# Gate and up projections of a two-block transformer forward pass: two weight units taken matmul by matmul in turn instead of one after the other

## What is computed

```
def swiglu(h, w1, w3, w2):
    return (jax.nn.silu(h @ w1) * (h @ w3)) @ w2
...
x = x + c * swiglu(rmsnorm(x, gain), w1, w3, w2)      # c is 1.0 once, 0.5 four times
```

## Time and profile before

| | |
|---|---|
| median of 3 runs | 3458.57 us (3454.5 to 3460.02) |
| the profiled execution | 3455.16 us |
| its span, first to last instruction | 3453.4 us |
| TensorE matmuls | 15598, busy 3324.4 us (96% of the span) |
| TensorE weight loads | 15598 |
| VectorE busy | 1727.2 us (50%) |
| ScalarE busy | 1109.7 us (32%) |
| mean share of DMA bandwidth (queue of the weights) | 25.2% of 16 engines |
| mean granted TensorE clock | 0.987 |

### The profile page before, as it was taken

The page is one execution under the profiler, slowest core; times in us unless marked ns, Lnnn a source line. Parts: engine busy times, 40 slices in busy tenths (PEclk is TensorE's granted clock), DMA queues, the critical chain, the costliest instruction groups (busy, mean ns, idle before and its releaser), DMA issues.

```text
span 3453.4 us, 41062 instructions
## 1 busy us (share of the span) xinstructions
PE 3324.4 (96%) x15598; PEld 2730.9 (79%) x15598; DVE 1727.2 (50%) x2510; ACT 1109.7 (32%) x1482; POOL 0.2 (0%) x4
## 2 busy tenths in 40 slices
PE   7989999989999999999899999999999989999998
PEld 6667777868888888888786888888888878778886
DVE  4554444555454455435755545444443576555543
ACT  3554444343222222222333322232222233332221
POOL 0000000000000000000000000000000000000000
PEclk9999999999999999999999999999999989999999
DMA  3222222313222222232231222222222223222222
GB/s 125 86 74 92 86 80 70 107 61 116 97 97 98 97 94 95 97 101 80 74 104 61 86 97 97 98 92 97 97 98 101 80 70 108 68 79 94 95 97 86
DMA packets 88829, 313.49 MB, mean 91 GB/s; under 512 B 9984, under 2 KB 10496, under 8 KB 88448
## 3 DMA queue, kind: packets, MB, share of 16 engines
q1 hardware_dynamic: 82080, 294.69, 25.2%
q10 hardware_dynamic: 6624, 17.03, 1.6%
HBM read 309.58 MB, written 2.10 MB: 90 GB/s over the span
## 4 chain that ended last, share of the span: by engine, by line
PE 89%; DVE 5%; ACT 3%; issue 2%; DMA 0%; ACTq 0%; DVEq 0%
PE ps L827 27%; PE ps L829 27%; PE ps L828 27%; PE ps L1026 1%; PE ps L889 1%; PE ps L944 1%; PE ps L898 1%; DVE wlo L1257 1%; ACT whi L1072 1%; PE ps L973 1%; PE ps L934 1%; PE ps L957 0%; PE ps L1056 0%; PE ps L926 0%; PE ps L977 0%
## 5 line engine op out<-in xcount | busy, mean ns | idle before, releaser
L827 PE MATMUL ps<-x_hi,whi 128*128 128x512 f32 x2816 | 1118.0, 397 | 13.1 <-DVE wlo L1257 13.1
L829 PE MATMUL ps<-x_hi,wlo 128*128 128x512 f32 x2816 | 1101.9, 391 | 0.0
L828 PE MATMUL ps<-x_lo,whi 128*128 128x512 f32 x2816 | 1101.6, 391 | 0.0
L1072 ACT ACTIVATE whi<-raw 128x1024 fp32r<-128x1024 f32 x554 | 583.0, 1055 | 985.8 <-DMA raw<-in_weights 983.3
L1257 DVE TENSOR_TENSOR wlo<-raw,whi 128x1024 fp32r<-128x1024 f32 x554 | 676.3, 1223 | 397.2 <-ACT whi L1072 388.9
L827 PEld LDWEIGHTS ps<-x_hi,whi 128*128 128x128 f32 x2816 | 533.1, 189 | 129.1 <-DVE wlo L1257 13.2
L829 PEld LDWEIGHTS ps<-x_hi,wlo 128*128 128x128 f32 x2816 | 532.1, 189 | 112.8
L828 PEld LDWEIGHTS ps<-x_lo,whi 128*128 128x128 f32 x2816 | 532.9, 189 | 110.5 <-issue 2.6
L827 PE MATMUL ps<-h_hi,whi 128*128 128x512 f32 x880 | 342.3, 389 | 0.0
L828 PE MATMUL ps<-h_lo,whi 128*128 128x512 f32 x880 | 342.3, 389 | 0.0
L829 PE MATMUL ps<-h_hi,wlo 128*128 128x512 f32 x880 | 342.3, 389 | 0.0
(11 more groups left out here) (253 smaller groups left out, 3038.7 us busy)
## 6 DMA issues: line engine op xcount, KB each, us to landing
raw<-in_weights SPq DMA_DIRECT2D x554, 512.0 KB, 3.2
bias<-in_biasB ACTq DMA_DIRECT2D x16, 384.0 KB, 3.2
bias<-in_biasA ACTq DMA_DIRECT2D x16, 256.0 KB, 3.1
x_res<-in_x SPq DMA_DIRECT2D x8, 256.0 KB, 6.3
x_res<-in_x ACTq DMA_DIRECT2D x1, 2048.0 KB, 8.5
out_x<-x_res SPq DMA_DIRECT2D x8, 256.0 KB, 2.0
mem_raw<-in_mem ACTq DMA_DIRECT2D x1, 1024.0 KB, 5.0
mem_raw2a<-in_mem ACTq DMA_DIRECT2D x2, 512.0 KB, 3.8
```

Of the source, the lines that this page charges most:

```text
L827: pe.matmul(out, hi, xhi, start=start, stop=False)
L828: pe.matmul(out, hi, xlo, start=False, stop=False)
L829: return pe.matmul(out, lo, xhi, start=False, stop=stop)
L1072: return act.activation(out, in_, ACT.Copy, scale=scale)
```

## The change

For every pair but pair 0 the order of the 48 matmuls is different. Before: 24 of the gate unit, then 24 of the up unit. After, for each of the 8 tiles k: gate and up with `whi` and `x_hi`; gate and up with `whi` and `x_lo`; gate and up with `wlo` and `x_hi`. The same matmuls are issued, with the same operands, and each bank gets its own in the same order. All waits of the pair (both units' `unit_ready`, both readers' `fg` and `fu`) now stand ahead of its first matmul, and both units raise `unit_free` at the pair's end, gate first. Pair 0 of each layer keeps the old order, with the norm's sum after its gate unit. No other engine's program is changed.

```
+                    def both(i, jj):
+                        pair = []
+                        for w, (name, first) in enumerate((("fg", fg0), ("fu", fu0))):
+                            c = 2 * jj + w
+                            pe.wait_ge(sems["unit_ready"], i * 4 + (u0 + c + 1))
+                            if not isinstance(i, int):
+                                pe.wait_ge(sems[name], i * 2 + (first + jj - 1))
+                            pair.append((PS[:, c, :], whi[(u0 + c) % RING], wlo[(u0 + c) % RING]))
+                        for k in range(DC):
+                            cc = slice(k * P, (k + 1) * P)
+                            for out, hi, _ in pair:
+                                pe.matmul(out, hi[:, cc], XH[:, k, :], start=(k == 0), stop=False)
+                            for out, hi, _ in pair:
+                                pe.matmul(out, hi[:, cc], XL[:, k, :], start=False, stop=False)
+                            for out, _, lo in pair:
+                                mm = pe.matmul(out, lo[:, cc], XH[:, k, :], start=False, stop=(k == DC - 1))
+                                if k == DC - 1:
+                                    mm.then_inc(sems["unit_free"], 1)
                     def gate_up(i):
                         for jj in range(2):
+                            if jj or not isinstance(i, int):
+                                both(i, jj)
+                                continue
                             for w, (name, first) in enumerate((("fg", fg0), ("fu", fu0))):
                                 c = 2 * jj + w
                                 pe.wait_ge(sems["unit_ready"], i * 4 + (u0 + c + 1))
-                                if not isinstance(i, int):
-                                    pe.wait_ge(sems[name], i * 2 + (first + jj - 1))
...
```

More of the change, by code:

```diff
@@ L991, in gate_up @@
                                 pe.wait_ge(sems["unit_ready"], i * 4 + (u0 + c + 1))
-                                if not isinstance(i, int):
-                                    pe.wait_ge(sems[name], i * 2 + (first + jj - 1))
                                 for k in range(DC):
-                                    if isinstance(i, int) and jj == 0 and w == 0:
+                                    if w == 0:
                                         pe.wait_ge(*on("xl", (n, k)))
```

## The result

| | before | after |
|---|---|---|
| median of 12 runs | 3456.89 us (3453.23 to 3460.02) | 3463.47 us (3459.3 to 3468.45) |
| ratio, 95% interval | | 1.0016 (1.0009 to 1.0024) |
| span of the profiled execution | 3453.4 us | 3465.2 us |

The changed kernel is slower by 0.16%. This ratio is the recorded estimate over all runs of both; the medians alone lie 6.6 us apart, which is 0.19%. The forecast was 3463 us and 0.16%.

A forecast was written before the change was run, and what follows sets the result against it. TensorE was taken as the bound, at 226.7 ns per matmul in the loop. 0 (pace) + 0 (loop) + 5 x 1.1 = 5.5 us gave 3460.7 or 3464.1 us; forecast 3463 us, range 3456 to 3472.

The forecast's parts named there:

- The pace: Reordered matmuls of all layers: starts stay 226.7 ns apart, so the reordering costs 0; bounds 67 us less or more.
- A: Reordered matmuls: part of the fixed 13.3 ns hangs on bank or weights; up to 67 us less, 3392 us; chance 0.06.
- B: Reordered matmuls: alternating destinations or weight tiles cost something; at 0.24 us a matmul, 3525 us; chance 0.05.
- The 215.7 ns: Distance between matmul starts at 512 columns by the skill page; reaching it would give 55 us less.
- The loop's waits: Waits now at each loop pair's start: both units ready with 2.2 us left, so cost 0.
- Rival D: Loop's feed comes late: each further 1 us costs 1 us in 20 pairs of five layers, 100 us, 3563; chance 0.05.
- The opening: Each layer's opening: pair 1 waits for both low parts; 1.05 to 1.13 us a layer, 5.5 us in five.
- rows 7: Late low part in the earlier trace: weight load 0.11 us after its end, second matmul 0.45 us after.
- rows 5: First layer's opening in the earlier trace: shortest wait, weight load 0.05 us after low part's end, giving a 1.07 us loss.
- Rival C: Openings: the 1.1 us stop takes the clock down, 1.7 us more each, 8.5 in all, 3472 us; chance 0.08.
- Rival E: Openings: low parts ready sooner or the wait absorbed, so the change does nothing, 3458 us; chance 0.08.

The follow-up runs named there:

- e7: Changed kernel, but both units of an interleaved pair accumulate into one bank, the gate's; 3467.55 us in one run.
- e8: Changed kernel, but both banks of an interleaved pair take the up unit's weights; 3464.04 us in one run.
- e5: Changed kernel, with each high part in the layers' loops made in 32 pieces of 32 columns; 3546.03 us, ratio 1.0261 to the kernel before.
- e1: Changed kernel with pair 1 of each layer back in the old order, the loop still interleaved; 3459.08 us, ratio 1.0003 to the kernel before.
- e2: Kernel before with only pair 1 of each layer interleaved, the loop in the old order; 3462.52 us, ratio 1.0017 to the kernel before.
- e4: Kernel before, old matmul order, but with all waits of a pair ahead of it; 3460.38 us, ratio 1.001 to the kernel before.
- e3: Changed kernel with pair 1's high parts ahead of the norm's root, low parts ahead of the reciprocal; 3459.5 us, ratio 0.9998 to the kernel before.
- e6: Kernel before, with each high part in the layers' loops made in 32 pieces of 32 columns; 3460.05 us, ratio 1.0008 to the kernel before.
- e9: Changed kernel, but loop matmuls take only the first 64 of 128 weight columns; 3478.12 us in one run.

## Why the prediction was right

*The pace.* It was costed at nothing, from two places where bank and weights changed together without a longer or a shorter distance. Measured: 226.67 ns in the changed kernel, and e7 and e8 take bank and weights apart. Rivals A and B fall. Taking one kind of transition, seen at two places, for 5040 was a risk; the new profile and e7 and e8 show that it was sound.

The 215.7 ns of the Trainium skill, "TensorE: Matmul & The Clock Gate", section "Wait — 56ns, not 53.3ns?", was not reached by any order of these fp32r products; the measurement decides, 226.67 ns.

*The loop's waits.* They were costed at nothing, with 2.2 us left. In the changed kernel the second low part is finished 5.5 us before the first weight load at the first pair of each loop, and 2.6 to 3.9 us before it at all the others. One pair in VectorE's and then in TensorE's timeline:
```profile
892.33 0.69 DVE L1501 TENSOR_TENSOR h_lo<-ffn_m,h_hi 128x512 f32 x1
893.98 2.51 DVE L1278 TENSOR_TENSOR wlo<-raw,whi 128x1024 fp32r<-128x1024 f32 x2 [0.95 <-ACT whi L1093]
...
900.17 0.41 PEld L999 LDWEIGHTS ps<-x_hi,whi 128*128 128x128 f32 x2
```
893.98 + 2.51 = 896.49, 3.7 us ahead of 900.17. I had taken 2.4 us for the second transfer's delay and added it whole; the second high part began 1.3 us after the first (892.88 and 894.16). The bound was on the safe side. Rival D's mechanism is real, but it is not at work in the changed kernel: e5 shows it at 91.5 us over before, once the feed is 5.4 us longer (7.75 us for both high parts, against 892.88 to 895.22, 2.34). Its rate was too high. It charged 1 us in each pair for each 1 us too late. In e5 the feed is 5.4 - 3.7 = 1.7 us too late, and the loss is 1.7 us in every second pair only.

*The opening.* The forecast was 1.05 to 1.13 us by layer, from the late low part set on the times of the earlier trace rows; measured 1.11 to 1.14. The figures of rows 7 were the right ones to carry over: the weight load came 0.12 us after the low parts' end (0.11 there, while the 0.05 of rows 5 did not come), and the second matmul of pair 1 came 0.45 us after it. e1 and e2 put the whole loss there, e4 shows that the wait makes it and not the order, and e3 that it goes when the low parts leave their place behind the reciprocal. Sum: 5.5 forecast, 5.6 us measured inside the layers.

*The clock.* Rival C forecast a fall after the stop. The windows of the new profile around the openings of all five layers stand at 1.00; the third and the last:
```profile
1963.00:1987.00 24.00, 23.11 (x102) 18.82 (x101) 15.32 (x17) 7.46 (x8) 0.00 (x0) 1.00 0.20 69
...
3095.00:3119.00 24.00, 23.11 (x102) 18.83 (x101) 16.27 (x17) 8.45 (x9) 0.00 (x0) 1.00 0.23 85
```
Rival C falls. The warning of the Trainium skill, "TensorE: Matmul & The Clock Gate", section "A second HAM failure mode: psum-queue depth-cycling", doesn't bear on this loop: it names small idles between groups as the cause, and here the loop has none: in the new profile no two starts of neighbours there are more than 227 ns apart.

*Rival E*, no cost at all, falls by the list of waits. The medians differ by 6.6 us, 1.0 more than the layers; the interval of the ratio, 3 to 8 us, holds both.

*What was luck.* The mechanism and its 5.5 us were worked out. The close match of the time was not, or not alone. The forecast's two figures don't fit each other: 3463 is 0.13% over the 3458.57 us of that time, and 0.16% is 5.5 us over it. The median of the kernel before then came out at 3456.89 with 12 runs; 5.5 us on top of it are 3462.4. That 3463.47 was measured owes about 1 us to scatter.

## What to carry to other kernels

Before reordering matmuls for the engine's sake, look in the trace for a place where the wished transition already occurs once; if its distance is the usual one, as it was here, there is little to hope for. Then go through the waits that the new order gathers: here the gathered waits cost nothing in the steady loop, which had slack, and they cost 1.1 us at each opening, where a reciprocal still stood ahead of the producer. The cure was to move the producer, two low parts ahead of a 3.35 us reciprocal (e3), and it brought the time back to that of the kernel before, not below it. And e5 and e6 show that a loss of slack can stay invisible in the time until the feed gets longer.

## What the runs showed of the hardware that I had not expected

With half the weight columns per matmul (e9) the weight load went from 188 to 135 ns, and the matmuls came further apart, 230.0 ns against 226.7. The fixed 13.3 ns a matmul of the fp32r products depends neither on bank (e7), nor on equal weights (e8), nor in that direction on the length of the load; what makes it is open. And the granted clock in one stretch of 7 us with short stops, the same code in both kernels, was 1.00 in one profile and 0.55 in another: that stretch alone moves a single execution by up to 3.2 us (0.45 x 7).
